# A hybrid encoder layer on one core: four phase borders of an RWKV-7 / attention / gated-convolution kernel, and the order of its gates phase

## The chip, the cores and the metric

One core of a Trainium2 chip. The metric is the device time of one execution in microseconds. A run of this kernel takes about 3.4 ms.

## The reference

The input is x of 2048 tokens by 1024 features, float32, one layer:

```python
h = rms_norm(x)
p = h @ w_in                       # columns: RWKV part (1792), attention part
# RWKV-7, both directions, 8 heads of 64
pf = p + mu_prev*(prev - p) + mu_next*(next - p)
r, k, v, xw, xa, xg = split(pf)
decay = exp(-exp(-softplus(-(w0 + tanh(xw) @ w2)) - 0.5))
iclr  = sigmoid(a0 + xa @ a2);  gate = sigmoid(xg) @ g2
kk = heads(k * k_k);  kk = kk * rsqrt(sum(kk*kk) + 1e-12)
kd = k * (1 + (iclr - 1) * k_a);  b = iclr * kk
S = S*w + (S a) b^T + v k^T;  y = S r     # over 2048 tokens, two directions
y  = group_norm(y_fwd + y_bwd) + bonus;  A = y * gate
# windowed attention (+-128), 8 query heads, 2 kv heads -> B
x = x + concat(A, B) @ w_out
u = conv3(rms_norm(x) @ w_up)      # 2 x 2816 columns, depthwise over tokens
x = x + (silu(u_gate) * u_value) @ w_down
```

## The kernel before

The kernel is a sequence of phases, each a function with its own block of five instruction streams (SyncE for transfers, TensorE, ScalarE, GpSimd, VectorE). Within a phase the order on each engine is written out by hand and the streams meet in counting semaphores (`done(engine, name, n)` waits until `name` has reached n). A phase ends in `end_phase` (L388), which clears its semaphores behind a barrier of all engines. The phases are `first_block` (norm, attention projection), `attention_block`, `rwkv_project_block`, `gates_block`, `recurrence_block`, `mix_block`, `up_block` and `down_block`. Tokens are the free axis nearly everywhere: TN = 4 quarters of NT = 512 tokens, with features on the 128 partitions; RU = 4 is the number of 128-feature tiles of the RWKV width and KD = 8 that of the model width. A matrix product is three float32r matmuls, high by high, low by high and high by low (L91 to L93).

**rwkv_project_block** (L608) makes 14 tiles of 128 columns, in pairs. TensorE does four quarters of a tile, ScalarE copies each quarter to `raw` (L694), VectorE forms the token shift with three operations over all 2048 tokens (L734, L737, L741) and SyncE stores the tile. The last pair holds xw/xa (tile 12) and xg (tile 13). Behind the last tile ScalarE issues eight loads of w0 into row 64 of `lora` (L702), takes tanh of xw and copies xa (L706, L707), and takes the sigmoid of xg (L709).

**gates_block** (L752) runs 32 items: four quarters n, two directions d, four feature tiles. For an item TensorE makes the decay product of a token tile (`p_tok`, L848), the iclr product (`p_iclr`, L851) and, one item later, the running sums of the sigmoids (`p_csum`, L838); ScalarE takes two sigmoids (L885, L889); VectorE makes `keep` (L960), kd (L940) and copies the sums out (L947); GpSimd makes b1 = iclr * kk (L917). `iclr` has three places. Once per quarter the key norm has to be made: GpSimd multiplies keys by k_k (`raw`, L901, 4 operations), ScalarE squares (L870), TensorE sums over heads in pairs (`sums`, L827), ScalarE takes Ln and Exp(-0.5 x) (`roots`, L872) and VectorE multiplies (`unit`, L930). `raw` stands at item 3 of a quarter for the next one, `square` at item 5, and sums, roots and unit at its last item. SyncE stores a quarter's groups in two transfers, 4 MB and 3 MB.

**recurrence_block** (L970) works on 32 chunks of 64 tokens in both directions. A slot c does the state part of chunk c and the preparing part of chunk c + 8. Per group of four chunks the inverses of triangular 32x32 blocks are found by substitution on GpSimd (`solve`, L1072 to L1096) in a transposed layout: VectorE turns the problems (L1480) and turns the results back with two stream transposes (`turn_back`, L1482 to L1487), whereupon ScalarE spreads them (`spread`, L1336). The VectorE order of a slot is a table of stages followed by `turn_back`. At the start VectorE clears buffers and eight PSUM banks (L1410 to L1415), and the other engines wait for all of it.

**mix_block** (L1526) goes in slots of one quarter n and one output tile m: the RWKV result is normed and gated, joined with the attention result, projected, added to x (L1887), stored, squared and summed over tiles on GpSimd (`gather`, L1820) for the next RMS norm (norm on TensorE L1706, root on ScalarE L1772, reciprocal on VectorE L1891). In the last quarter's slots it begins the up phase: SyncE loads quarters 0 and 1 of x back (`load_next`, L1630) into `x_next`, which lies in mix's buffer y; GpSimd scales the eight tiles of a quarter with the reciprocal norm (L1833); ScalarE and VectorE split them into high and low (L1798, L1910, L1914); TensorE makes the first up products of quarter 0 (`up_ahead`, L1717). SyncE loads quarters 2 and 3 in `up_block` (L1965), where GpSimd scales them (L2026).

**up_block** (L1923) takes 22 pairs of a gate tile and a value tile: TensorE four quarters each, ScalarE copies (L2051) and the gate's SiLU (L2057), VectorE three taps per tile (L2108, L2111, L2114), the gate product (L2119) and the value product (L2122), SyncE the store (L1971). **down_block** loads these back.

The wait of ScalarE in the gates is the place that the ring of three sets:

```python
done(act, "iclr_lora", g + 1)
done(act, "b1", g - 2)
done(act, "keep", g - 2)
nc.scalar.activation(iclr[:, g % 3], p_iclr[:, g % 2], ACT.Sigmoid,
                     bias=K.vec("a0", d * RU + j)).then_inc(S["iclr"], 1)
```

## Time and profile before

| | |
|---|---|
| median of 3 runs | 3365.49 us (3362.63 to 3369.56) |
| the profiled execution | 3360.1 us |
| its span | 3358.3 us |
| mean granted clock of TensorE | 0.962 |
| busy, TensorE / VectorE / ScalarE / GpSimd | 91% / 47% / 32% / 23% |
| gates: first VectorE row, last VectorE row | 813.9, 936.2 us |
| recurrence: first VectorE row | 949.3 us |
| up: first matmul | 1886.4 us |
| up: last store | 2861.7 us |

The page's first part gives the busy shares of the whole span; since TensorE is the busiest engine by far, the places to look at are its holes. The part in tenths gives their position by slice of 84 us:

```profile
PE   7878989997847999997899699999999999799999
DVE  4555543333857565543644544444444444333333
ACT  4435541113623444433334221211111121222222
POOL 4434530000625667741224500000000000000000
PEclk9989999998968999998999899999999999899999
DMA  3331122331785333323464211111111111621221
```

### The profile page before, as it was taken

What the parts mean: (1) busy time and instruction counts of PE and PEld (TensorE: products, weight loads), DVE (VectorE), ACT (ScalarE), POOL (GpSimd) and SP (SyncE); (2) the same over time, 40 slices, a digit from 0 to 9 for tenths busy, and PEclk for the clock granted to TensorE, in tenths of its full rate; (3) what the DMA queues carried; (4) which work ended last, traced back from release to release, by engine and by line L of the source; (5) the groups of instructions that cost most, each with busy time, mean ns of one, the idle gap of its engine ahead of it and who ended that gap; (6) DMA issues with size and microseconds to landing.
All of it is one profiled execution on the core that took longest, in us unless ns stands there. A gap on an engine that the chain in (4) does not pass through costs nothing. (4 is left out here: it accounts for less than half of the span.)

```text
span 3358.3 us, 63150 instructions
## 1 busy us (share of the span) xinstructions
PE 3047.4 (91%) x26252; PEld 2446.2 (73%) x26252; DVE 1571.7 (47%) x2023; ACT 1059.4 (32%) x2009; POOL 768.0 (23%) x873
## 2 busy tenths in 40 slices
PE   7878989997847999997899699999999999799999
PEld 4554448885536899996566578888888887688887
DVE  4555543333857565543644544444444444333333
ACT  4435541113623444433334221211111121222222
POOL 4434530000625667741224500000000000000000
PEclk9989999998968999998999899999999999899999
DMA  3331122331785333323464211111111111621221
GB/s 113 132 86 36 38 53 63 75 75 39 286 260 154 114 111 117 99 90 102 157 204 141 91 57 45 49 50 50 50 47 37 47 50 38 247 100 47 99 98 35
DMA packets 229906, 317.57 MB, mean 95 GB/s; under 512 B 80473, under 2 KB 155737, under 8 KB 226738
## 3 DMA queue, kind: packets, MB, share of 16 engines
q1 hardware_dynamic: 223634, 308.98, 28.8%
q10 hardware_dynamic: 6048, 5.38, 0.5%
q8 instruction: 167, 2.74, 0.3%
q14 instruction: 57, 0.47, 0.0%
HBM read 211.17 MB, written 103.14 MB: 94 GB/s over the span
## 5 line engine op out<-in xcount | busy, mean ns | idle before, releaser
L91 PE MATMUL up_p<-h_hi,up_w_hi 128*128 128x512 f32 x1408 | 551.8, 392 | 13.5 <-DVE h_lo L2098 8.2
L92 PE MATMUL up_p<-h_lo,up_w_hi 128*128 128x512 f32 x1408 | 550.2, 391 | 0.0
L93 PE MATMUL up_p<-h_hi,up_w_lo 128*128 128x512 f32 x1408 | 550.2, 391 | 0.0
L2051 ACT COPY up_raw<-up_p 128x512 f32<-128x512 f32 x176 | 103.2, 588 | 758.6 <-PE up_p L93 750.1
L91 PEld LDWEIGHTS up_p<-h_hi,up_w_hi 128*128 128x128 f32 x1408 | 266.0, 189 | 71.2 <-issue 13.2
L92 PEld LDWEIGHTS up_p<-h_lo,up_w_hi 128*128 128x128 f32 x1408 | 266.0, 189 | 56.0 <-issue 0.5
L93 PEld LDWEIGHTS up_p<-h_hi,up_w_lo 128*128 128x128 f32 x1408 | 265.7, 189 | 55.4
L2108 DVE TENSOR_SCALAR up_con<-up_raw,vecs_sb 128x2048 f32<-128x2048 f32 x44 | 59.3, 1347 | 515.8 <-ACT up_raw L2051 515.8
L91 PE MATMUL down_p<-down_act_hi,down_w_hi 128*128 128x512 f32 x704 | 274.6, 390 | 23.5 <-DVE down_act_lo L2252 23.5
L92 PE MATMUL down_p<-down_act_lo,down_w_hi 128*128 128x512 f32 x704 | 274.3, 390 | 0.0
L93 PE MATMUL down_p<-down_act_hi,down_w_lo 128*128 128x512 f32 x704 | 274.3, 390 | 0.0
L2249 DVE TENSOR_TENSOR down_w_lo<-down_w,down_w_hi 128x1024 fp32r<-128x1024 f32 x88 | 107.7, 1224 | 309.8 <-ACT down_w_hi L2231 309.8
L2231 ACT CAST down_w_hi<-down_w 128x1024 fp32r<-128x1024 f32 x88 | 92.8, 1055 | 353.2 <-PE down_p L93 334.6
L91 PE MATMUL p_rwkv<-h_hi,rwkv_project_w_hi 128*128 128x512 f32 x448 | 175.2, 391 | 10.2 <-DVE rwkv_project_w_lo L716 10.2
L92 PE MATMUL p_rwkv<-h_lo,rwkv_project_w_hi 128*128 128x512 f32 x448 | 175.0, 391 | 0.0
L93 PE MATMUL p_rwkv<-h_hi,rwkv_project_w_lo 128*128 128x512 f32 x448 | 175.0, 391 | 0.0
L91 PEld LDWEIGHTS down_p<-down_act_hi,down_w_hi 128*128 128x128 f32 x704 | 132.5, 188 | 51.3 <-issue 23.9
L92 PEld LDWEIGHTS down_p<-down_act_lo,down_w_hi 128*128 128x128 f32 x704 | 132.5, 188 | 27.7
L93 PEld LDWEIGHTS down_p<-down_act_hi,down_w_lo 128*128 128x128 f32 x704 | 132.4, 188 | 27.5
L529 POOL TENSOR_SCALAR attention_prob<-attention_prob,attention_inv 128x384 f32<-128x384 f32 (+1 forms) x96 | 117.1, 1236 | 120.6 <-DVE attention_inv L595 120.6
L584 DVE CUSTOM_DVE_ANT_0 attention_s<-attention_p_s,attention_bias,attention_nsink 128x384 f32<-128x384 f32 (+1 forms) x128 | 75.9, 594 | 108.5 <-PE attention_p_s L492 89.3
L1094 POOL TENSOR_TENSOR rec_V<-rec_V,rec_part 128x31 f32<-128x31 f32 (+15 forms) x217 | 122.2, 563 | 17.0
(244 smaller groups left out, 6324.4 us busy)
## 6 DMA issues: line engine op xcount, KB each, us to landing
rec_inp<-gate_chunks SPq DMA_DIRECT2D x64, 512.0 KB, 3.6
act_out<-up_con SPq DMA_DIRECT2D x22, 1024.0 KB, 4.3
down_act<-act_out SPq DMA_DIRECT2D x88, 256.0 KB, 2.8
up_w<-in_w_up SPq DMA_DIRECT2D x42, 512.0 KB, 4.0
gate_chunks<-gates_out SPq DMA_DIRECT2D x4, 4096.0 KB, 11.8
first_w<-in_w_attn SPq DMA_DIRECT2D x24, 512.0 KB, 3.9
rkv_chunks<-rwkv_project_mix SPq DMA_DIRECT2D x12, 1024.0 KB, 6.5
gate_chunks<-gates_out SPq DMA_DIRECT2D x4, 3072.0 KB, 12.3
```

Source lines behind the costliest of these rows:

```text
L91: pe.matmul(out, w_hi, x_hi, start=start, stop=False)
L92: pe.matmul(out, w_hi, x_lo, start=False, stop=False)
L93: return pe.matmul(out, w_lo, x_hi, start=False, stop=stop)
L529: ops.tensor_scalar(prob[:, i % PB, lo:hi], prob[:, i % PB, lo:hi], inv[:, b % 2, h:h + 1], None, ALU.mult).then_inc(S[name], 1)
L584: nc.vector.tensor_tensor_reduce(s_sb[:, h, lo:hi], p_s[:, i % 3, lo:hi], bias[:, h, lo:hi], 1.0, nsink[:, h:h + 1], ALU.add, ALU.min, lea ...
L1094: op = ops.tensor_tensor(V[:, below, cols], V[:, below, cols], product, ALU.add)
L2051: nc.scalar.copy(raw[:, half, 1 + n * NT:1 + (n + 1) * NT], p_u[:, half, n]).then_inc(S["copied_" + c], 1)
L2108: nc.vector.tensor_scalar(con[:, half], raw[:, half, 1:T + 1], cw(1, half, j), cb(half, j), ALU.mult, ALU.add).then_inc(S["c0" + c], 1)
L2231: nc.scalar.copy(w_hi[:, k % 2], w[:, k]).then_inc(S["w_hi"], 1)
L2249: nc.vector.tensor_tensor(w_lo[:, k % 2], w[:, k], w_hi[:, k % 2].bitcast(F32), ALU.subtract).then_inc(S["w_lo"], 1)
```

## The change

It touches six places.

1. **Projection.** The eight w0 loads are issued by SyncE at the phase's start. Tanh and the copy of xw/xa stand on ScalarE behind the second quarter's copy of tile 13. The shift of tile 13 is done in two pieces, tokens 0 to 1534 and 1535 to 2047, and written to `K.xg` itself; its sigmoid moves to the gates, in four pieces at items 0 to 3.
2. **Gates.** GpSimd squares (one 128x2048 product per quarter), `iclr` has nine places, and fixed tables say at which item the next quarter's key norm is worked on. The ones row is set and copied for the first quarter first and for the rest at item 1. Exp follows each Ln by pairs. The first quarter is saved in seven transfers.
3. **Recurrence, start.** GpSimd clears ring_g, low and side; VectorE clears dec and then the banks, in the order 2, 3, 0, 1; ScalarE waits for dec alone.
4. **Recurrence, turn-back.** `turn_back` stands in front of `state` and `state_decay` in VectorE's slot.
5. **Mix to up.** `x_next` lies in `up_con`; SyncE loads quarter 0 ahead of the slot's store, quarter 1 a slot earlier and quarter 2 still in mix; tiles k with k % 4 < 2 are scaled by GpSimd, the others by VectorE.
6. **Up.** The last pair's value tile is filtered, multiplied and stored in the same two pieces; the SiLU stands in front of the last quarter's copy.

```diff
# rwkv_project_block
+                        if last and b == 1 and n == 1:
+                            act.wait_ge(S["mixed20"], R_TILES // 2)
+                            nc.scalar.activation(K.xw[0:64, :], mix[0:64, 0], ACT.Tanh).then_inc(S["lora_copied"], 1)
+                            nc.scalar.copy(K.xw[64:128, :], mix[64:128, 0]).then_inc(S["lora_copied"], 1)
...
+                    if last and b:
+                        mixed(g, b, m, K.xg, slice(0, T - NT - 1), TN - 1, 1)
+                        mixed(g, b, m, K.xg, slice(T - NT - 1, T), TN, 2)
+                    else:
+                        mixed(g, b, m, mix[:, b], slice(0, T), TN, 1, not first)
# gates_block
-    RAW, SQUARE = 3, 5
+    RAW_AT = {0: 1, ITEMS + 3: 2, 2 * ITEMS + 3: 3}
+    ROOTS_AT = {4: 0, ITEMS + 2: 1, 2 * ITEMS - 1: 2, 3 * ITEMS - 1: 3}
+    SUMS_AT = {5: 0, ITEMS + 2: 1, 2 * ITEMS - 1: 2, 3 * ITEMS - 1: 3}
+    UNIT_AT = {6: 0, ITEMS + 2: 1, 2 * ITEMS - 1: 2, 3 * ITEMS - 1: 3}
+    IRING = 9
...
-                    if i == SQUARE and n + 1 < TN:
-                        square(n + 1)
...
-                    done(act, "b1", g - 2)
-                    done(act, "keep", g - 2)
+                    done(act, "b1", g - IRING + 1)
+                    done(act, "keep", g - IRING + 1)
...
+                    if g < TN:
+                        nc.scalar.activation(K.xg[:, g * NT:(g + 1) * NT], K.xg[:, g * NT:(g + 1) * NT], ACT.Sigmoid)
+                    if g in ROOTS_AT:
                         act.preload_act_table_set("natural_log_exp_and_others")
-                        roots(0)
...
+                        roots(ROOTS_AT[g])
...
                     op.then_inc(S["kk"], 1)
+                    done(pool, "kk", n + 1)
+                    nc.gpsimd.tensor_tensor(inv[:, :, :], kk[:, :, :], kk[:, :, :], ALU.mult).then_inc(S["sq"], 1)
...
-                nc.vector.memset(row[64:128, :], 1.0).then_inc(S["ones"], 1)
+                nc.vector.memset(row[64:128, 0:NT], 1.0).then_inc(S["ones"], 1)
# recurrence_block
-                act.wait_ge(G["init"], INIT)
+                act.wait_ge(G["dec_set"], 2)
...
+                for d in DIRS:
+                    nc.gpsimd.memset(ring_g[d][:, :, :, 0:BL], 0.0).then_inc(G["init"], 1)
+                    nc.gpsimd.memset(low[d][:, :, :], 0.0).then_inc(G["init"], 1)
+                    nc.gpsimd.memset(side[d][:, :, :], 0.0).then_inc(G["init"], 1)
...
-                                         (ahead, rb_mask, c + 1), (carry, state, c), (carry, state_decay, c)):
+                                         (ahead, rb_mask, c + 1)):
...
                         turn_back((c + 1) // GROUP)
-                    for go, stage, n in ((front, diagonal_a, c + LAG), (front, diagonal_b, c + LAG)):
+                    for go, stage, n in ((carry, state, c), (carry, state_decay, c),
+                                         (front, diagonal_a, c + LAG), (front, diagonal_b, c + LAG)):
# mix_block
-        x_next = y.rearrange("p j c m t -> p (j c m t)").rearrange("p (k t) -> p k t", t=NT)
+        x_next = K.up_con.rearrange("p h t -> p (h t)").rearrange("p (k t) -> p k t", t=NT)
...
-                    if s == AHEAD + 4:
+                    if s == AHEAD + 3:
                         done(sp, "h0_lo", KD)
                         load_next(1)
+                for i in range(2):
+                    done(sp, "h1_lo", 4 * i + 4)
+                    sp.dma_start(x_next[:, 4 * i:4 * i + 4],
+                                 K.x2_dram.rearrange("m p t -> p m t")[:, 4 * i:4 * i + 4, toks(2)]).then_inc(
+                        K.rows_in[f"in{i}"], 16)
...
+                    if s == SLOTS - 1:
+                        for k in range(KD):
+                            if k % 4 >= 2:
+                                scale(1, k)
# up_block
+                            if last and half and n == TN - 1:
+                                gate(j)
                             take(half, j, n)
-                    gate(j)
+                    if not last:
+                        gate(j)
...
+                    gated(j)
+                    if last:
+                        for nth, (at, quarters) in enumerate(((EARLY, TN - 1), (LATE, TN)), 1):
+                            taps(1, j, at, quarters, nth)
+                            product_out(j, at, nth)
```

GpSimd's order in the gates, before (L905 is the product with k_k, L917 is b1):

```order
L905 TENSOR_TENSOR gates_kk<-gates_keys,vecs_sb 128x512 x4
L917 TENSOR_TENSOR gates_out<-gates_iclr,gates_out 128x8x64 x3
L905 TENSOR_TENSOR gates_kk<-gates_keys,vecs_sb 128x512 x4
L917 TENSOR_TENSOR gates_out<-gates_iclr,gates_out 128x8x64 x8
L905 TENSOR_TENSOR gates_kk<-gates_keys,vecs_sb 128x512 x4
L917 TENSOR_TENSOR gates_out<-gates_iclr,gates_out 128x8x64 x8
L905 TENSOR_TENSOR gates_kk<-gates_keys,vecs_sb 128x512 x4
L917 TENSOR_TENSOR gates_out<-gates_iclr,gates_out 128x8x64 x13
```

and with the change (L925 the product, L930 the square, L939 b1):

```order
L925 TENSOR_TENSOR gates_kk<-gates_keys,vecs_sb 128x512 x4
L930 TENSOR_TENSOR gates_inv<-gates_kk 128x2048
L925 TENSOR_TENSOR gates_kk<-gates_keys,vecs_sb 128x512 x4
L930 TENSOR_TENSOR gates_inv<-gates_kk 128x2048
L939 TENSOR_TENSOR gates_out<-gates_iclr,gates_out 128x8x64 x11
L925 TENSOR_TENSOR gates_kk<-gates_keys,vecs_sb 128x512 x4
L930 TENSOR_TENSOR gates_inv<-gates_kk 128x2048
L939 TENSOR_TENSOR gates_out<-gates_iclr,gates_out 128x8x64 x8
L925 TENSOR_TENSOR gates_kk<-gates_keys,vecs_sb 128x512 x4
L930 TENSOR_TENSOR gates_inv<-gates_kk 128x2048
L939 TENSOR_TENSOR gates_out<-gates_iclr,gates_out 128x8x64 x13
```

The second group's product and square now stand in front of the first b1, and four squares are new.

VectorE in a slot of the recurrence with a turn-back, before:

```order
L1433 TENSOR_TENSOR rec_akrk<-rec_bank,rec_masks 128x512 x2
L1439 TENSOR_TENSOR rec_rb<-rec_bank,rec_masks 128x256 x2
L1453 TENSOR_TENSOR rec_H<-rec_bank,rec_H 128x256 x2
L1460 TENSOR_TENSOR rec_H<-rec_H,rec_dec_end 128x256 x2
L1486 STREAM_TRANSPOSE rec_upper<-rec_V 128x32x32
L1487 STREAM_TRANSPOSE rec_lower<-rec_V 128x32x32
L1466 TENSOR_SCALAR rec_E<-rec_bank,rec_masks 128x128 x2
```

and with the change:

```order
L1457 TENSOR_TENSOR rec_akrk<-rec_bank,rec_masks 128x512 x2
L1463 TENSOR_TENSOR rec_rb<-rec_bank,rec_masks 128x256 x2
L1510 STREAM_TRANSPOSE rec_upper<-rec_V 128x32x32
L1511 STREAM_TRANSPOSE rec_lower<-rec_V 128x32x32
L1477 TENSOR_TENSOR rec_H<-rec_bank,rec_H 128x256 x2
L1484 TENSOR_TENSOR rec_H<-rec_H,rec_dec_end 128x256 x2
L1490 TENSOR_SCALAR rec_E<-rec_bank,rec_masks 128x128 x2
```

The two transposes changed places with the state's four operations.

VectorE at the end of mix, before (L1887 adds x, L1910 and L1914 make the low parts, L1891 is the reciprocal):

```order
L1891 RECIPROCAL inv_all<-inv_all 128x512
L1887 TENSOR_TENSOR mix_x<-mix_p_out,mix_x 128x512 x3
L1910 SCALAR_TENSOR_TENSOR h_lo<-mix_y,vecs_sb,h_hi 128x512 x4
L1896 TENSOR_TENSOR up_w_lo<-up_w,up_w_hi 128x1024
L1887 TENSOR_TENSOR mix_x<-mix_p_out,mix_x 128x512
L1910 SCALAR_TENSOR_TENSOR h_lo<-mix_y,vecs_sb,h_hi 128x512 x4
L1896 TENSOR_TENSOR up_w_lo<-up_w,up_w_hi 128x1024
L1887 TENSOR_TENSOR mix_x<-mix_p_out,mix_x 128x512 x2
L1914 SCALAR_TENSOR_TENSOR h_lo<-mix_y,vecs_sb,h_hi 128x512 x8
L1891 RECIPROCAL inv_all<-inv_all 128x512
```

and the last part of it with the change (L1925 adds x, L1930 scales):

```order
L1961 SCALAR_TENSOR_TENSOR h_lo<-up_con,vecs_sb,h_hi 128x512 x4
L1925 TENSOR_TENSOR mix_x<-mix_p_out,mix_x 128x512
L1961 SCALAR_TENSOR_TENSOR h_lo<-up_con,vecs_sb,h_hi 128x512 x4
L1944 TENSOR_TENSOR up_w_lo<-up_w,up_w_hi 128x1024
L1925 TENSOR_TENSOR mix_x<-mix_p_out,mix_x 128x512
L1944 TENSOR_TENSOR up_w_lo<-up_w,up_w_hi 128x1024
L1925 TENSOR_TENSOR mix_x<-mix_p_out,mix_x 128x512
L1930 TENSOR_TENSOR up_con<-up_con,inv_all 128x512 x4
L1925 TENSOR_TENSOR mix_x<-mix_p_out,mix_x 128x512
L1965 SCALAR_TENSOR_TENSOR h_lo<-up_con,vecs_sb,h_hi 128x512 x8
L1935 RECIPROCAL inv_all<-inv_all 128x512
```

The four scales of quarter 1 stand on VectorE in front of the last addition of x.

## Rows read from the trace of the kernel before

**Rows 1.** Windows view: busy us (instructions) by engine, granted clock, DMA share, GB/s; gates, recurrence.

```profile
817.00:941.00 124.00, 104.23 (x416) 60.31 (x416) 94.12 (x114) 72.85 (x88) 67.52 (x48) 0.95 0.64 245
1060.00:1565.00 505.00, 474.03 (x14638) 465.55 (x14632) 263.13 (x558) 209.88 (x632) 308.73 (x529) 0.99 0.32 100
```

**Rows 2.** Timeline, end of the projection: start us, us, instruction, [idle before <-releaser].

```profile
800.40 0.59 ACT L694 COPY rwkv_project_raw_pad<-p_rwkv 128x512 f32<-128x512 f32 x1 [4.85 <-PE p_rwkv L93]
800.41 5.14 ACTq L702 DMA_DIRECT2D lora<-in_vecs  x8
804.73 2.35 DVE L741 SCALAR_TENSOR_TENSOR rwkv_project_mix<-rwkv_project_raw_pad,vecs_sb,rwkv_project_mix 128x2048 f32<-128x2048 f32 x1
810.74 1.91 ACT L709 ACTIVATE xg<-rwkv_project_mix 128x2048 f32<-128x2048 f32 x1
```

**Rows 3.** Timeline, start of the gates.

```profile
813.93 1.76 DVE L922 MEMSET gates_row<- 64x2048 f32 x1 [6.85 <-PEq L391]
817.37 1.22 PE L848 MATMUL gates_p_tok<-lora,gates_row 128*128 128x512 f32 x1 [17.01 <-DVE gates_row L928]
```

**Rows 4.** Gates: tile views (duration ns min/median/max) and timeline of TensorE.

```profile
L905 POOL TENSOR_TENSOR gates_kk<-gates_keys,vecs_sb x16: 1040/1217/1487, 819.3 to 899.3; 128x512 f32<-128x512 f32 x16
L917 POOL TENSOR_TENSOR gates_out<-gates_iclr,gates_out x32: 1266/1452/1727, 836.8 to 933.5; 128x512 f32<-128x512 f32 x32
L960 DVE TENSOR_SCALAR gates_keep<-gates_iclr,vecs_sb,gates_less x32: 535/886/1481, 836.6 to 936.2; 128x512 f32<-128x512 f32 x32
...
849.46 1.05 PE L838 MATMUL gates_p_csum<-gates_tri,gates_sig 128*128 128x128 f32 x8
852.07 1.05 PE L838 MATMUL gates_p_csum<-gates_tri,gates_sig 128*128 128x128 f32 x8
```

**Rows 5.** Timeline, start of the recurrence, ACT and TensorE.

```profile
957.39 1.28 ACT L1322 ACT_TABLE_LOAD   x1 [24.02 <-DVE rec_bank L1415]
981.83 1.12 PE L1195 MATMUL rec_bank<-consts_sb,rec_toks 64*64 64x64 f32 x16 [5.41 <-DMA rec_toks<-rkv_chunks]
```

**Rows 6.** Timeline, a slot of the recurrence with a turn-back.

```profile
1106.45 0.25 POOL L1094 TENSOR_TENSOR rec_V<-rec_V,rec_part 128x31 f32<-128x31 f32 x1
1106.60 0.89 DVE L1439 TENSOR_TENSOR rec_rb<-rec_bank,rec_masks 128x256 f32<-128x256 f32 x2 [0.71 <-PE rec_bank L1184]
1111.74 2.01 DVE L1487 STREAM_TRANSPOSE rec_lower<-rec_V 128x1024 f32<-128x1024 f32 x1
1114.83 0.66 PE L1184 MATMUL rec_bank<-rec_side,rec_g 64*64 64x32 f32 x16 [1.12 <-ACT rec_side L1345]
1115.70 0.48 PE L1184 MATMUL rec_bank<-rec_Z,rec_g 64*64 64x32 f32 x10 [0.22 <-ACT rec_side L1345]
```

**Rows 7.** Timeline, end of mix and first wait of up.

```profile
1860.99 12.51 POOL L1833 TENSOR_TENSOR mix_y<-mix_y,inv_all 128x512 f32<-128x512 f32 x8 [4.55 <-DMA mix_y<-x_dram]
1875.23 1.22 PE L1706 MATMUL mix_p_total<-mix_total,consts_sb 128*128 128x512 f32 x1 [15.00 <-POOL mix_total L1820]
1878.06 3.35 DVE L1891 RECIPROCAL inv_all<-inv_all 128x512 f32<-128x512 f32 x1 [2.34 <-ACT inv_all L1772]
1886.42 0.47 PE L91 MATMUL up_p<-h_hi,up_w_hi 128*128 128x512 f32 x1 [2.29 <-DVEq L2087]
1891.41 1.29 POOL L2026 TENSOR_TENSOR up_con<-up_con,inv_all 128x512 f32<-128x512 f32 x1 [16.24 <-DMA up_con<-x_dram]
1906.67 0.77 PE L91 MATMUL up_p<-h_hi,up_w_hi 128*128 128x512 f32 x1 [7.49 <-DVE h_lo L2098]
```

**Rows 8.** Timeline, end of up, and the page's DMA issues (KB each, median us to landing).

```profile
2851.06 1.35 DVE L2108 TENSOR_SCALAR up_con<-up_raw,vecs_sb 128x2048 f32<-128x2048 f32 x1 [15.64 <-ACT up_raw L2051]
2861.74 0.35 SPq L1971 DMA_DIRECT2D act_out<-up_con  x1
2873.86 0.79 PE L91 MATMUL down_p<-down_act_hi,down_w_hi 128*128 128x512 f32 x1 [23.45 <-DVE down_act_lo L2252]
act_out<-up_con SPq DMA_DIRECT2D x22, 1024.0 KB, 4.3
```

More of the change, by code:

```diff
@@ L865, in _ @@
                               K.d["masks"][:, at:at + 2 * P]).then_inc(S["w_in"], 16)
-                def square(n):
-                    done(act, "kk", n + 1)
-                    done(act, "kn", n)
-                    nc.scalar.activation(inv[:, :, :], kk[:, :, :], ACT.Square).then_inc(S["sq"], 1)
                 def roots(n):
@@ L916, in _ @@
                     out_free(pool, n)
-                    nc.gpsimd.tensor_tensor(out[:, n % 2, :, group(f"b1_{d}") + u, :], by_chunk(iclr[:, g % 3]),
+                    nc.gpsimd.tensor_tensor(out[:, n % 2, :, group(f"b1_{d}") + u, :], by_chunk(iclr[:, g % IRING]),
                                             out[:, n % 2, :, group("kk") + u, :], ALU.mult).then_inc(S["b1"], 1)
@@ L951, in _ @@
                 dve.wait_ge(S["less"], 1)
-                for n in range(TN):
-                    copy_row(n)
+                copy_row(0)
                 for g, (n, i, d, u) in enumerate(items):
-                    if g == 0:
-                        sums_out(0, *items[0])
-                        unit(0)
+                    if g == 1:
+                        nc.vector.memset(row[64:128, NT:], 1.0).then_inc(S["ones"], 1)
+                        for m in range(1, TN):
+                            copy_row(m)
+                    if i == 0:
+                        dve.wait_ge(S[f"k_in{n % 2}"], 16 * (n // 2 + 1))
                     done(dve, "iclr", g + 1)
                     done(dve, "kd", g - 1)
-                    nc.vector.tensor_scalar(keep[:, g % 2], iclr[:, g % 3], K.vec("k_a", u), less[:, u:u + 1],
+                    nc.vector.tensor_scalar(keep[:, g % 2], iclr[:, g % IRING], K.vec("k_a", u), less[:, u:u + 1],
                                             ALU.mult, ALU.add).then_inc(S["keep"], 1)
                     times_k(g, n, i, d, u)
-                    if g >= 1:
-                        sums_out(g, n, i, d, u)
-                    if i == ITEMS - 1 and n + 1 < TN:
-                        unit(n + 1)
+                    sums_out(g, n, i, d, u)
+                    if g in UNIT_AT:
+                        unit(UNIT_AT[g])
         end_phase(nc, S)
@@ L1784, in _ @@
                     stage(s, square)
-                    for k in ahead(s, 2):
+                    for k in ahead(s, 1):
                         done(act, "with_bonus", TN * RU)
-                        done(act, "x0_scaled", k + 1)
+                        scaled_ahead(act, 0, k)
                         nc.scalar.activation(K.h0_hi[:, k], x_next[:, k], ACT.Copy,
@@ L1907, in _ @@
                     stage(s, centre)
-                    for k in ahead(s, 3):
+                    for k in ahead(s, 1):
+                        if k % 4 >= 2:
+                            scale(0, k)
+                    for k in ahead(s, 2):
                         done(dve, "h0_hi", k + 1)
```

209 lines of the change are left out of this document (119 added, 90 removed).

## The prediction

> **What bounds the kernel now.** I read the page's tenths by slice first, then the windows view of the stretches that the change touches, then the timeline around each place where TensorE sits idle. The profiled execution took 3360.1 us (span 3358.3), 5.4 us under the median of the three runs shown, 3365.49; I add the sum up against the profiled execution and carry the difference over. TensorE is busy 91% of the span, so what can be won lies in its holes. In the recurrence its matmuls cover 474 of 505 us, in the gates 104 of 124 us [rows 1], and at the border of mix and up it stands still for 15.00 us [rows 7]. The changed borders stand on the chain in full: phases end in a barrier.
>
> **Projection to gates.** The last copy stands at 800.40, 4.85 us behind the one before, and DVE filters the last tile from 801.0 to 804.73 + 2.35 = 807.1. Meanwhile ACT issues eight small loads for 5.14 us, then does tanh, a copy, a table load and the sigmoid, which ends at 810.74 + 1.91 = 812.65 [rows 2], and gates begins 1.3 us behind it [rows 3]. The change issues the loads at the start on SP, where the first tiles' loads stand behind 5.14 us of issuing; a tile is over 20 us of TensorE, which covers it. Tanh and copy move to the last tile, behind its second quarter's copy: 3.8 us on ACT between copies 5.44 us apart (4.85 + 0.59). Three quarters of the taps are done ahead of the last copy (4.5 us within the same 5.44); behind it stand 513 columns, 6.1/4 = 1.5 us and some 0.15. DVE ends near 802.65 in place of ACT at 812.65: **-10.0 us**. The sigmoid of xg goes into gates as four pieces of 0.6 us on ACT.
>
> **Gates.** The first matmul waits for the ones and four row copies, 3.4 us behind DVE's start [rows 3]; a quarter of the memset and one copy leave about 1.1, so it begins 2.1 us earlier. From there an item costs TensorE 2.61 us (852.07 - 849.46), and the 32 items take (936.2 - 836.6)/31 = 3.2 us each [rows 4], because ACT's squares and roots stand between items. If nothing waited, 32 x 2.61 = 83.5, four groups of sums at about 4.6 (two pairs of matmuls with ACT's logarithm between) and 5 us at the ends give 107 against 124 now: 17 us to be had at best. But the squares go to GpSimd as one 128x2048 operation. The rows of before have none; the nearest ones are the key product at 1.04 to 1.49 us and b1 at 1.27 to 1.73 us per 512 columns, undisturbed at the lower ends [rows 4]. Four times these bounds the square by 4.2 and 6.9; I take 4.9, since most of its time has no partner on DVE in the first and last groups. GpSimd then has, per group, 8 x 1.45 + 4 x 1.22 + 4.9 = 21.4 us of work in 26, but in a fixed order, and the order makes waits. By hand from the block's start: the roots of group 0 come behind item 4, and TensorE waits 2.4 us at item 6; the nine places of the iclr ring are full at item 9, so ACT waits there for b1 of item 0, which stands on GpSimd behind the second group's key product and square (34 + 5 + 4.9 = 44 us into the block), about 4 us; b1 then runs behind by about ten items, so the square of group 2, behind 11 of them, is ready near 71 where TensorE wants it near 64, 7 us. Group 3 has room. 107 + 2.4 + 4 + 7 + about 3 for blocking on DVE is 123: **-1 us**, with ends -12 (the b1 at its lowest 1.27, waits of 7 gone) and +8 (b1 at 1.73). The Trainium skill, "SBUF — State Buffer", section "SBUF: two separate sides", says that the port pair of GpSimd and VectorE is an exclusive lock for the whole instruction. The trace is softer for 512 columns: keep is 0.54 us alone, 0.89 at the median and 1.48 at most [rows 4], which fits waiting for the end of one GpSimd operation. By the rule each square would hold DVE for 4.9 us, where I have counted 0.7; that is the rival below. "GPSIMD Engine Reference", section 3.1, gives 4497 ns for a tensor_tensor of 2048 float32 columns; by it the square would cost 0.4 us less than mine, which no run here shows yet.
> The last store's tail, and with it the recurrence's start, hang on the same last item: nothing more there.
>
> **Recurrence, start.** ACT's first step waits for all memsets on DVE and begins at 957.39 [rows 5]. Now it waits for two of 0.07 us, and the others are shared with GpSimd. The input it reads lands about 953 to 954: -3.3 us. A few us on, TensorE waits 5.41 us for a DMA of token rows [rows 5], whose round trips pace these slots; they are also released earlier, so I keep **-3.3**, ends -4 and 0.
>
> **Recurrence, turn-back.** At each of the seven groups' ends DVE transposes 1.96 and 2.01 us behind the state; ACT's spread needs both and TensorE waits 1.12 + 0.22 us for it [rows 6]. In front of the state the transposes could begin when GpSimd has the solve (1106.45 + 0.25) and DVE the masks (1106.60 + 0.89 = 1107.49); they end 2.3 us earlier, at 1111.5 instead of 1111.74 + 2.01. The spread then waits for ACT's y copy only (1112.2), in time. The state ends 3.3 us later, at 1112.9, and the next slot wants it at 1118.4. 7 x 1.34 = **-9.4 us**, rounded down to -9.1 for the tail of the copies; ends -11 and 0.
>
> **Mix to up.** GpSimd scales eight tiles alone (12.51 us from 1860.99 on, after its load), TensorE stands idle 15.00 us until the last gather lets the norm go at 1875.23, DVE's reciprocal is at 1878.06 + 3.35 and up begins at 1886.42 [rows 7]. The load now goes to the buffer of up_con and needn't wait for mix's y; it is issued a slot earlier (about 10 us, of which the slot's work takes some). The scales are split by two engines, four each, and on GpSimd 4 x 1.56 = 6.3 us that lie beside the last slots. TensorE's matmuls end 15.00 us ahead of 1875.23, at 1860.2. I let the gather be done by then and the norm (1.1 us) go at once, the leftover up matmuls run to 1866.6, the reciprocal end at 1868 and up start at 1869.1: **-17.3**. GpSimd then starts the third quarter's scales at once, as its rows are loaded before the barrier; before it waited 16.24 us for them and TensorE 7.49 [rows 7]. Its chain begins 5.0 us earlier after up's start (1891.41 - 1886.42): **-5.0**, together -22.3, ends -25 (all of 7.49 goes) and -15 (DVE's own scales hold its reciprocal back).
>
> **Up to down.** The last pair's filter is a chain on DVE behind the last copy, from 2851.06 to the store at 2861.74; the first down matmul comes at 2873.86, 12.1 us behind the store's issue, of which a store of 1024 KB takes 4.3 us to land [rows 8]. The copies are 5.44 us apart. Now ACT's gate (1.91 us) stands between the third quarter's copy, which ends at 2845.6, and the last one: it ends at 2847.5, DVE's product with it (2.3) at 2849.8, three quarters of the taps (6.05 x 3/4 = 4.5) at 2854.3, their product (1.7) at 2856.0, and the 513 columns behind them take 2.1 + 0.3: 2858.4, a gain of 3.3. The last store is a quarter of the bytes; how much sooner it lands no row shows, between 0 and 4.3 x 3/4 = 3.2 us; I take 1.2. **-4.5**, ends -6.5 and -3.3.
>
> **The sum.** -10.0 - 1 - 3.3 - 9.1 - 22.3 - 4.5 = -50.2 us: 3360.1 - 50.2 = 3309.9 profiled, 3365.5 - 50.2 = **3315** as a median.
>
> **The rivals.** (a) The waits in gates don't arise, because GpSimd runs near its lower ends (b1 1.27, square 4.2): gates gives 11 instead of 1, 3305. For it: alone, the operations are that short [rows 4]. Against it: DVE is busy 94 of the 124 us [rows 1], so GpSimd is seldom alone. Chance 0.20. (b) The square takes the ports for its whole length: four times about 4 us of DVE more, on the path in two or three of them, and b1 later by as much: +8 instead of -1, 3324. For it: keep's spread of 0.54 to 1.48. Against: no row has DVE held for longer than one operation of 512 columns, and the next square falls into DVE's slack. The skill's lock rule from above is this case. Chance 0.15. (c) The recurrence passes nothing on: the start is paced by the DMA's round trips, and the wait for the transposes comes back as one for the state. 12.4 us lost: 3327.6. For it: the 5.41 us wait [rows 5]. Against: after the transposes the state has 5 us to spare. Chance 0.10. (d) The other side: the solve on GpSimd. In front of the state, the transposes hold the state and its decay behind the solve, whose last step ends at 1106.45 + 0.25 [rows 6], 0.8 us ahead of the moment when DVE wants it. Were the solve late, every us beyond 0.8 + 4.2 (the state's slack) would be one on the path, seven times, for GpSimd's order is unchanged. To eat 50.2 us it must be late by 5 + 1.3 + 50.2/7 = 13.5 us in each group; by 14.5 it gives 3373. Nothing in the trace delays it so far (309 of 505 us busy on GpSimd [rows 1]): 0.02. That the change doesn't do what it says is no case of its own: the order on each engine shows every move.
>
> **How the numbers follow.** The forecast, 3315, has 0.53; (a) 0.20, (b) 0.15, (c) 0.10, (d) 0.02. The ends of single terms (mix and up, 7 us to the bad and 4 to the good, gates between) widen each by about 6. From 3301 to 3329 lie the forecast, (a) but for its outer part, (b) and most of (c): a little over 8 in 10. A measurement of this kernel tells apart about 0.2%, 6.7 us. Only a loss of 45 us beyond the forecast would bring it there: same 0.02, slower 0.03, faster 0.95.
>
> **What would show it.** In the profile after: gates' first DVE row near 803.9; in gates a GpSimd row of 128x2048 x4 near 4.9 us, ACT or TensorE waiting at item 9 and before the third sums, and a length near 123; no TensorE wait for the spread of over 0.5 us behind a turn-back, and slots without one as long as before; the idle stretch at mix and up at 1 to 3 us and the first wait of up below 3; the last store of up near 7.4 us behind the last copy's end. Wrong it would be if gates takes under 115 or over 130, if the solve's end moves with the transposes, or if DVE's reciprocal stands behind its scales.

## The result and the profile after

| | before | after |
|---|---|---|
| median | 3365.49 us (5 runs, 3355.24 to 3370.78) | 3338.19 us (5 runs, 3332.21 to 3338.81) |
| profiled execution (span) | 3360.1 (3358.3) | 3333.1 (3331.3) |
| mean granted clock | 0.962 | 0.965 |

The medians lie 27 us apart; the ratio is 0.9924 with a 95% interval of 0.9908 to 0.9939, so the time fell by 0.76%. The forecast was 50 us, and the result lies 9 us above the upper end of its range. Split at rows that both traces have, the profiled executions stand so:

| stretch | before | after | difference | forecast |
|---|---|---|---|---|
| start to the projection's last copy | 800.4 | 801.2 | +0.8 | 0 |
| last copy to gates' first VectorE row | 13.5 | 3.7 | -9.9 | -10.0 |
| that row to the recurrence's first | 135.3 | 153.4 | **+18.1** | -1 |
| that row to the last y copy | 615.0 | 601.1 | -14.0 | -12.4 |
| last y copy to up's first matmul | 322.1 | 310.0 | -12.1 | -17.3 |
| up's first matmul to down's | 987.5 | 977.0 | -10.4 | -9.5 |
| the rest | 484.4 | 485.0 | +0.6 | 0 |

One row is wrong by 19 us, of a miss of 23. The first rows are the projection's end on VectorE. Its last piece of 513 tokens now ends at 803.85, where ScalarE's sigmoid ended at 812.65 [rows 2], and gates begins 1 us behind it, at 804.83 instead of 813.93 [rows 3]:

```profile
803.10 0.75 DVE L748 SCALAR_TENSOR_TENSOR xg<-rwkv_project_raw_pad,vecs_sb,xg 128x513 f32<-128x513 f32 x1
804.83 0.48 DVE L944 MEMSET gates_row<- 64x512 f32 x1 [0.98 <-PEq L391]
```

The windows view of gates, columns as in [rows 1]:

```profile
804.00:947.00 143.00, 113.34 (x416) 63.38 (x416) 101.69 (x119) 70.62 (x93) 81.12 (x52) 0.89 0.58 209
```

Against [rows 1] TensorE does the same 416 matmuls in 113.3 instead of 104.2 us, at a mean granted clock of 0.89 instead of 0.95, and 29.7 us without a matmul stand where there were 19.8. Half of this growth of 19 us are waits, and the other half matmuls behind them at the lower of the clock's two levels, 1.2 instead of 2.4 GHz (from 883.1 to 891.4 us the mean granted clock is 0.52). The longer waits of TensorE on its timeline:

```profile
821.72 1.13 PE L867 MATMUL gates_p_csum<-gates_tri,gates_sig 128*128 128x128 f32 x8 [2.62 <-DVE gates_out L969]
836.27 1.91 PE L867 MATMUL gates_p_csum<-gates_tri,gates_sig 128*128 128x128 f32 x8 [2.49 <-ACT gates_sig L907]
853.99 3.44 PE L860 MATMUL gates_p_ss<-gates_inv,consts_sb 128*128 128x512 f32 x4 [4.46 <-POOL gates_inv L930]
859.63 3.08 PE L860 MATMUL gates_p_ss<-gates_inv,consts_sb 128*128 128x512 f32 x4 [2.20 <-ACT gates_inv L898]
883.03 3.78 PE L860 MATMUL gates_p_ss<-gates_inv,consts_sb 128*128 128x512 f32 x4 [6.67 <-POOL gates_inv L930]
888.02 3.50 PE L860 MATMUL gates_p_ss<-gates_inv,consts_sb 128*128 128x512 f32 x4 [1.21 <-ACT gates_inv L898]
913.87 1.13 PE L867 MATMUL gates_p_csum<-gates_tri,gates_sig 128*128 128x128 f32 x8 [2.23 <-DVE gates_out L969]
```

They name three engines. The sums at 853.99 and 883.03 waited for the square on GpSimd (4.46 and 6.67 us), and the rows behind a wait show the clock: eight running-sum matmuls in 1.91 us at 836.27 where a row at full clock has 1.05 [rows 4], four sums in 3.44 to 3.78 where one at full clock takes 1.98. Two of ScalarE's long waits are for the sums of the first quarter, and in front of item 9's sigmoid for a free place in the ring:

```profile
828.91 1.11 ACT L898 ACTIVATE gates_inv<-gates_p_ss,vecs_sb 128x1024 f32<-128x1024 f32 x1 [7.78 <-PE gates_p_ss L860]
855.24 0.69 ACT L911 ACTIVATE gates_iclr<-gates_p_iclr,vecs_sb 128x512 f32<-128x512 f32 x1 [9.44 <-POOL gates_out L939]
```

VectorE in the same phase:

```profile
810.45 1.37 DVE L984 TENSOR_SCALAR gates_keep<-gates_iclr,vecs_sb,gates_less 128x512 f32<-128x512 f32 x1 [4.48 <-DMA gates_keys<-rkv_chunks]
815.62 4.17 DVE L950 COPY gates_row<-xw 64x512 f32<-64x512 f32 x3
880.04 3.22 DVE L984 TENSOR_SCALAR gates_keep<-gates_iclr,vecs_sb,gates_less 128x512 f32<-128x512 f32 x1
908.24 3.22 DVE L984 TENSOR_SCALAR gates_keep<-gates_iclr,vecs_sb,gates_less 128x512 f32<-128x512 f32 x1
```

The first keep waits 4.48 us for the keys' load, with item 0's running sums, which TensorE needs two items later, queued behind it. Of the three late row copies, which the profile merges into one row, the first takes 3.51 us and the other two 0.41 each; the early one took 0.42. The long one begins 0.4 us behind the first square (815.24 to 818.84). Two keeps of normally 0.54 us, begun beside the third and the fourth square, take 3.22 each. So in three of the four squares one VectorE operation is held until the square is over, and two of TensorE's waits, 2.62 us at 821.72 and 2.23 at 913.87, are for running sums that VectorE copies out behind such an operation. GpSimd's order, the middle of the phase:

```profile
844.98 5.28 POOL L925 TENSOR_TENSOR gates_kk<-gates_keys,vecs_sb 128x512 f32<-128x512 f32 x4 [26.14 <-DVE gates_out L956]
850.34 3.60 POOL L930 TENSOR_TENSOR gates_inv<-gates_kk 128x2048 f32<-128x2048 f32 x1
853.89 11.10 POOL L939 TENSOR_TENSOR gates_out<-gates_iclr,gates_out 128x512 f32<-128x512 f32 x8
869.20 4.53 POOL L939 TENSOR_TENSOR gates_out<-gates_iclr,gates_out 128x512 f32<-128x512 f32 x3 [4.21 <-DVE gates_out L956]
873.68 5.29 POOL L925 TENSOR_TENSOR gates_kk<-gates_keys,vecs_sb 128x512 f32<-128x512 f32 x4
879.05 3.93 POOL L930 TENSOR_TENSOR gates_inv<-gates_kk 128x2048 f32<-128x2048 f32 x1
```

The square takes 3.60 to 3.93 us, less than either end of my estimate. But product, square and eight b1 come in that order, the first b1 starts 49 us into the phase, and the third product at 873.68 has eleven b1 in front of it.

At mix and up, the rows are of GpSimd, TensorE, VectorE and twice TensorE:

```profile
1850.39 6.88 POOL L1850 TENSOR_TENSOR up_con<-up_con,inv_all 128x512 f32<-128x512 f32 x4 [1.93 <-DMA up_con<-x_dram]
1858.80 1.12 PE L1741 MATMUL mix_p_total<-mix_total,consts_sb 128*128 128x512 f32 x2 [2.23 <-POOL mix_total L1861]
1863.86 3.34 DVE L1935 RECIPROCAL inv_all<-inv_all 128x512 f32<-128x512 f32 x1
1869.27 0.47 PE L91 MATMUL up_p<-h_hi,up_w_hi 128*128 128x512 f32 x1 [3.87 <-DVEq L2147]
1897.43 0.47 PE L91 MATMUL up_p<-h_hi,up_w_hi 128*128 128x512 f32 x1 [3.66 <-DVE h_lo L2158]
```

[rows 7] had 15.00 us of waiting for the gather, now it is 2.23; the reciprocal, ready to go near 1863.0, starts at 1863.86 behind eight low parts, and up's first long wait is 3.66 us instead of 7.49. At the end of up (ScalarE, VectorE, TensorE) the first down matmul comes 18.3 us behind the last copy's end, against 22.8 in [rows 8]:

```profile
2827.41 0.59 ACT L2108 COPY up_raw<-up_p 128x512 f32<-128x512 f32 x1 [3.04 <-PE up_p L93]
2835.39 0.69 DVE L2186 TENSOR_TENSOR up_con<-up_con 128x513 f32<-128x513 f32 x1
2846.30 0.79 PE L91 MATMUL down_p<-down_act_hi,down_w_hi 128*128 128x512 f32 x1 [18.93 <-DVE down_act_lo L2324]
```

### The profile page after: what moved, and what is told of

The parts are those of the page before. It is cut to its first block and busy times, and to the rows that moved or that the text cites. A ratio compares the mean times of both kernels' runs of the same rounds, so it can differ in the third digit from the quotient of the medians.

```text
span 3331.3 us, 63159 instructions
## 1 busy us (share of the span) xinstructions
PE 3048.5 (92%) x26252; PEld 2443.2 (73%) x26252; DVE 1575.8 (47%) x2033; ACT 1053.2 (32%) x2012; POOL 774.0 (23%) x875
## 5 line engine op out<-in xcount | busy, mean ns | idle before, releaser
L2170 DVE TENSOR_SCALAR up_con<-up_raw,vecs_sb 128x2048 f32<-128x2048 f32 (+2 forms) x45 | 59.5, 1323 | 497.9 <-ACT up_raw L2108 497.8
## 6 DMA issues: line engine op xcount, KB each, us to landing
down_w<-in_w_down SPq DMA_DIRECT2D x22, 512.0 KB, 13.5
```

The lines of the kernel that those rows point to most:

```text
L2170: nc.vector.tensor_scalar(con[:, half, at], raw[:, half, here], cw(1, half, j), cb(half, j), ALU.mult, ALU.add).then_inc(S["c0" + c], 1)
```

## The experiments

Theory **order**: the tables of the new gates phase make GpSimd, ScalarE and TensorE wait for each other in a loop (product, square, sums, roots, unit, next product), and the square is but one link. Theory **square**: the long GpSimd operation, with its hold on VectorE, costs this in any place. In front of both stood the question whether the phase is at fault at all. Phase lengths below are from the start of VectorE's first gates row to the end of its last (before 124.2, after 142.3 us); the 936.2 us that the section on the profile before gives for the last row are the start of the last keep, and the last row ends at 938.1. The kernel before was measured again beside each group of experiments: 3358.95 us beside e1 to e4, 3356.95 beside e5 to e8, 3358.51 beside e9 to e11 and 3361.75 beside e12, up to 8.5 us below the 3365.49 beside the changed kernel. Between groups, therefore, the ratios are compared and not the microseconds.

**e1, the old gates phase in the changed kernel.** `gates_block` of before, with one addition:

```diff
+                    if g < TN:
+                        nc.scalar.activation(K.xg[:, g * NT:(g + 1) * NT], K.xg[:, g * NT:(g + 1) * NT], ACT.Sigmoid)
```

> The changed kernel with the gates phase of before put back (the sigmoid of xg added in four pieces). If the new gates phase is what went wrong, the time falls by the 18 us by which that phase grew (142.3 instead of 124.2 us from its first VectorE row to its last): 3338 - 18 = 3320 us, and the phase lasts 124 to 127. Rival: the phase is long for something that stands outside it (earlier start, transfers of the phase before, the clock): then it stays near 140 with the old order too, and the time at 3335 to 3338.

Measured 3319.24 us, ratio 0.9880 (0.9861 to 0.9898); phase 125.8 us. The window of it:

```profile
805.00:930.00 125.00, 105.17 (x416) 60.79 (x416) 95.81 (x118) 75.94 (x93) 67.88 (x48) 0.95 0.63 238
```

The clock is back at 0.95 and the matmuls at 105 us. The other five parts are worth 1.20%, 40 us of the 3358.95 measured beside it (34 to 47 by the interval), 9 less than the forecast's 49. The new gates phase costs the difference of the two ratios, 0.44% or 15 us.

**e2, the new gates phase alone**, in the kernel before (without the sigmoid of xg, which stays in its projection).

> The kernel before with the new gates phase alone. Same two theories: if the phase itself costs 18 us, 3365.5 + 18 = 3383 us (a us or two less, since its keys are loaded in the same way); if the cost comes from the border in front of it, 3365.

Measured 3377.03 us, ratio 1.0060 (1.0041 to 1.0079), slower than before: 18 us above the 3358.95 beside it, as the first theory said; phase 137.6 us. The phase itself costs, 13 of the 18 us of its length even without the earlier border.

**e3, squares on ScalarE, all else as changed.**

```diff
+    SQUARE_AT = {3: 0, ITEMS + 1: 1, 2 * ITEMS - 1: 2, 3 * ITEMS - 1: 3}
...
+                    if g in SQUARE_AT:
+                        square(SQUARE_AT[g])
...
-                    nc.gpsimd.tensor_tensor(inv[:, :, :], kk[:, :, :], kk[:, :, :], ALU.mult).then_inc(S["sq"], 1)
```

> The changed kernel with the squares back on ScalarE (1.9 us each, in front of items 3, 9, 15 and 23), all else in the new gates phase as it is. Theory 'order' (the tables make GpSimd, ScalarE and TensorE wait for each other; the square only lengthens one link): two to three of four groups gain the difference 3.7 - 1.9 and the first b1 comes 3.7 us sooner, so 5 to 8 us off, phase 134 to 137, 3331 us. Theory 'square' (the long GpSimd operation with its hold on VectorE's port is the cause): nearly all 18 us go, phase 124 to 127, 3320 us.

Measured 3322.17 us, ratio 0.9887 (0.9870 to 0.9904); phase 127.8 us, 14.5 less: more than the difference of two durations, twice what "order" said and 0.8 us from what "square" said.

```profile
804.00:931.00 127.00, 107.35 (x416) 61.57 (x416) 92.84 (x119) 76.74 (x97) 66.52 (x48) 0.93 0.65 235
```

**e4, other tables, squares on GpSimd.**

```diff
+    RAW_AT = {0: 1, 8: 2, 16: 3}
+    ROOTS_AT = {4: 0, 11: 1, 18: 2, 25: 3}
+    SUMS_AT = {4: 0, 11: 1, 18: 2, 25: 3}
+    UNIT_AT = {4: 0, 11: 1, 18: 2, 25: 3}
...
+                    if n == 1:
+                        done(sp, "kd", 2 * ITEMS)
+                        done(sp, "kk", 2)
+                        load(3)
...
-                    if g == 1:
+                    if g == 0:
+                        sums_out(0, *items[0])
+                    if g == 5:
                         nc.vector.memset(row[64:128, NT:], 1.0).then_inc(S["ones"], 1)
...
```

> The changed kernel, squares on GpSimd as they are, other numbers in the tables: the products with k_k directly behind the b1 that they need (items 0, 8, 16), sums, roots and unit at items 4, 11, 18, 25, the three later row copies at item 5 instead of 1, item 0's sums copied first, the fourth quarter's keys loaded as soon as their place is free. Theory 'order': with the waits gone the phase lasts 115 to 122 us, 20 to 27 less: 3311 to 3318 us. Theory 'square': the squares cost the same in any place, the phase stays above 135: 3330 us or more.

Measured 3321.05 us, ratio 0.9887 (0.9871 to 0.9904); phase 126.3 us, 16 less, between the two expectations. All four squares are on GpSimd here, and each still holds one VectorE operation, so the hold alone is not the cause. Either mending alone takes nearly all of the loss: it was the squares in that order. The windows view shows the new bound, VectorE with 109.5 of 126 us, and the tile view of its operations (duration ns min/median/max) why:

```profile
806.00:932.00 126.00, 104.68 (x416) 59.90 (x416) 109.54 (x119) 70.64 (x93) 83.47 (x52) 0.95 0.63 230
```

```profile
L988 DVE TENSOR_SCALAR gates_keep<-gates_iclr,vecs_sb,gates_less x32: 535/880/3819, 813.9 to 930.3; 128x512 f32<-128x512 f32 x32
L963 DVE TENSOR_TENSOR gates_out<-gates_keep,gates_keys x32: 691/1636/3972, 814.8 to 930.9; 128x512 f32<-128x512 f32 x32
```

A keep of 0.54 us lasts up to 3.82 and a kd of 0.69 up to 3.97 us: as long as one whole square (3.66 to 3.93 us here). The copies of the running sums, whose source is in PSUM (where TensorE's results stand), stay at 0.68 to 0.69 us in every run. The Trainium skill, "SBUF — State Buffer", section "SBUF: two separate sides", calls the port pair that VectorE and GpSimd share an exclusive lock for the whole instruction; these rows agree with it.

**e5 and e6, the new tables in halves** (one execution each, so their phases are compared and not their times): e5 is e4's change at the start of the phase (roots, sums, unit of quarter 0 at items 3, 4, 4; the row copies at item 5), e6 its products at items 8 and 16 with the earlier load.

> The changed kernel with the start of the gates alone mended: roots, sums and unit of the first quarter at items 3, 4 and 4 instead of 4, 5 and 6, the later row copies at item 5, item 0's sums copied first; the products with k_k of quarters 2 and 3 stay at items 11 and 19. Theory 'order': the first unit comes 8 to 10 us earlier (it began 37.5 us into the phase), the later links are unchanged, so the phase of 142 us loses 8 to 10: 132 to 134. Theory 'square' (each square costs its length wherever it stands): unchanged within 3 us.

> The changed kernel with the products and squares of quarters 2 and 3 moved from items 11 and 19 to items 8 and 16 (three b1 of 4.5 us earlier), and the fourth quarter's keys loaded as soon as their place is free. Theory 'order': the waits for the squares of quarters 2 and 3 (6.7 us of TensorE, and ScalarE behind it) shrink by 4.5 us each: phase 133 to 136. Theory 'square': unchanged within 3 us.

Measured 3330.88 us with a phase of 138.7, and 3315.7 us with a phase of 134.4 (e6 had the shortest recurrence of all, see below). TensorE's wait for the third square stays in e5 (first row) and shrinks in e6 (second row):

```profile
880.71 3.78 PE L860 MATMUL gates_p_ss<-gates_inv,consts_sb 128*128 128x512 f32 x4 [6.53 <-POOL gates_inv L930]
```

```profile
874.88 1.98 PE L861 MATMUL gates_p_ss<-gates_inv,consts_sb 128*128 128x512 f32 x4 [1.91 <-POOL gates_inv L931]
```

e5 gained 3.6 of the 8 to 10 us expected, nearer to what "square" said. The first unit came 28 us into the phase instead of 38, but the square of quarter 1 then held a keep for 3.81 us, and TensorE waited 6.48 us for the running sums behind it, in place of 4.46 for the square itself; the third square's wait was untouched. e6 gained 8, as "order" expected. Together they give 11.5, and e4, which also moves sums and roots, 16.

**e7, each square in four pieces** (one execution):

```diff
-                    nc.gpsimd.tensor_tensor(inv[:, :, :], kk[:, :, :], kk[:, :, :], ALU.mult).then_inc(S["sq"], 1)
+                    for u in range(RU):
+                        op = nc.gpsimd.tensor_tensor(inv[:, u], kk[:, u], kk[:, u], ALU.mult)
+                    op.then_inc(S["sq"], 1)
```

> The changed kernel with each square in four GpSimd operations of 512 columns. If VectorE is held for the length of one GpSimd operation, its longest keep falls from 3.22 us to at most 1.5 us; GpSimd itself gets slower (4 x 1.1 to 1.3 = 4.4 to 5.2 instead of 3.6 to 3.9). Theory 'order': the chain through the square is 1 us longer, phase 142 to 146. Theory 'square' by its hold on the port: phase 130 to 136.

Measured 3324.93 us, phase 138.6 us: neither range. The longest keep is 1.37 us, so the hold is one operation long. GpSimd's four pieces take 4.0 to 5.2 us together, and TensorE's waits for the second and third squares grow from 4.46 and 6.67 to 4.89 and 7.58 us. The phase is 3.7 us shorter all the same, which fits a shorter hold: the 2.23 us wait in front of the last sums is gone, and TensorE's matmuls take 110.5 instead of 113.3 us; the early wait of 2.62 us stays, at 2.83. By this one execution the hold is a small share of the 18 us.

```profile
L986 DVE TENSOR_SCALAR gates_keep<-gates_iclr,vecs_sb,gates_less x32: 536/660/1370, 810.1 to 941.0; 128x512 f32<-128x512 f32 x32
L931 POOL TENSOR_TENSOR gates_inv<-gates_kk x16: 1036/1216/1482, 814.9 to 910.8; 128x512 f32<-128x512 f32 x16
```

**e8, new tables and squares on ScalarE** (in front of items 3, 10, 17, 24).

> The new tables (products at items 0, 8, 16; sums, roots, unit at 4, 11, 18, 25) with the squares on ScalarE in front of items 3, 10, 17, 24. With the tables and the squares on GpSimd the phase took 126.3 us with VectorE busy 109.5 of them, held for up to 3.97 us by a square. Theory 'VectorE is the bound there, lengthened by the squares': 4 x 3 us less of it, phase 114 to 120, 3308 to 3314 us. Rival: ScalarE, which must wait for the product before it can square, takes the gain back: 124 to 128, 3319 to 3323 us.

Measured 3312.36 us (3301.44 to 3318.08), ratio 0.9859 (0.9831 to 0.9887); phase 120.5 us, half a us above the first expectation, with a time inside it. It has the lowest ratio of all and beats both kernels; from e1, whose interval overlaps its own, it can't be told.

```profile
804.00:925.00 121.00, 105.47 (x416) 60.98 (x416) 96.59 (x119) 76.95 (x97) 68.16 (x48) 0.94 0.68 248
```

**e9, the turn-back behind the state again**, on e1: the two stages back in the first table.

> The kernel of e1 (all of the change but the gates phase; 3319 us) with the two transposes back behind the state. Theory 'the order of the turn-back is worth its TensorE wait': waits for the spread 13 us again instead of 6, the stretch from the first y to the last back from about 490 to about 499 us, 3328 us. Rival: the shorter stretch is scatter from run to run (it lay between 484 and 497 us with the same code): no more than 3 us, 3319 to 3322.

Measured 3324.65 us, ratio 0.9901 (0.9878 to 0.9923); e1's 0.9880 lies inside this interval. The stretch from first y to last y is 498.3 us (e1 490.8, before 502.0), as the first theory said. Who waits for the spread's tile (us, times), in the changed kernel and in e9:

```profile
  PE rec_bank L1207: 6.1, 1
```

```profile
  PE rec_bank L1193: 13.1, 12
```

The one wait left is the first group's, before the steady slots. One pair of executions can't tell 7 us here from scatter, but the profiles taken together do better: the three with the turn-back behind the state (before, e2, e9) have 502.0, 496.1 and 498.3 us, mean 498.8, and the eleven with it in front 484.3 to 497.0, mean 490.7. The 8 us between the means fit the 7 us of waits that are gone.

**e10, the recurrence's start as before**, on e1.

> The kernel of e1 with the recurrence's start as before (all clearing on VectorE, everybody waits for it). Theory 'the start passes on': the first decay step is 3.5 to 4.3 us later behind VectorE's first row, and the first y as much: 3322 to 3323 us. Rival: the loads of token rows pace the first slots and swallow it: the first y stands at the same distance, 3319.

Measured 3318.63 us, ratio 0.9880 (0.9859 to 0.9901), the same as e1. Behind the first row of the recurrence the first decay step comes at 9.4 us (e1 7.1), the first y at 111.4 (110.7): of 2.4 us 0.7 are left, and TensorE waits five times for token rows in these slots either way (3.4 to 6.2 us each). By this pair the rival was right. But e1 has the latest first y of the eleven profiles with the new start, which lie at 108.2 to 110.7 us, mean 109.4; the three with the old start (before, e2, e10) have 113.0, 113.3 and 111.4, mean 112.6. So the start passes on some 2 to 3 us, too little for the time of a whole execution to show.

**e11, all sixteen scales on GpSimd**, on e1.

```diff
-                        if k % 4 < 2:
-                            scale(0, k)
+                        scale(0, k)
```

(the same for quarter 1; VectorE's are dropped)

> The kernel of e1 with all sixteen scales of quarters 0 and 1 back on GpSimd; buffer, loads and all else stay. It tells the earlier load from the sharing: if the load brought the 12 us at this border, they stay (from the last y to up's first matmul 309 to 311 us, 3319); if the sharing did, the stretch grows by four scales of GpSimd, some 6 us, to 316 (3325).

Measured 3331.57 us, ratio 0.9916 (0.9896 to 0.9936). The stretch from last y to up is 315.4 us (e1 309.8), and TensorE waits for the gather again:

```profile
1838.51 12.59 POOL L1835 TENSOR_TENSOR up_con<-up_con,inv_all 128x512 f32<-128x512 f32 x8 [2.31 <-DMA up_con<-x_dram]
1852.82 2.08 PE L1726 MATMUL mix_p_total<-mix_total,consts_sb 128*128 128x512 f32 x2 [10.34 <-POOL mix_total L1846]
```

12.59 us for eight scales in a row, as before; 10.34 us of waiting instead of 15.00. Of the 12 us won at this border, 5.6 are the sharing and the rest, by subtraction, the earlier load. The whole rose by 12 us against e1 and by 13 against e10, measured beside it, 7 more than this stretch shows: 2.0 to 2.4 each in front of the gates, in the recurrence and in up, of which the first two have the same code and are scatter.

**e12, half of the running sums copied by ScalarE**, on e8: items of odd number, with a semaphore for each engine.

```diff
-                    done(pe, "csum_out", g - 1)
+                    done(pe, f"csum_out{g % 2}", g // 2)
...
+            copy = nc.scalar.copy if g % 2 else nc.vector.tensor_copy
```

> The kernel of e8 (new tables, squares on ScalarE; phase 120.5 us, 3312 us) with the running sums of every second item copied out by ScalarE instead of VectorE: 16 x 0.68 = 11 us less for VectorE, 10 more for ScalarE. If VectorE sets the steady item of 2.9 us there, the phase falls to 113 to 117 us and the time to 3305 to 3309. Rival: ScalarE with roots, squares and copies becomes the bound and the phase stays at 119 to 124, 3311 to 3316.

Measured 3320.24 us, ratio 0.9879 (0.9862 to 0.9895), which overlaps e8's: the two can't be told apart. The phase fell to 116.9 us as expected, but the recurrence starts 131.3 us behind the phase's first row, in e8 132.0. Windows of its end:

```profile
910.00:920.00 10.00, 9.16 (x48) 6.10 (x47) 9.86 (x11) 5.89 (x10) 7.63 (x6) 1.00 1.02 401
920.00:930.00 10.00, 0.00 (x0) 0.00 (x0) 1.74 (x3) 0.00 (x0) 0.00 (x0) 0.60 1.02 402
930.00:936.00 6.00, 0.00 (x0) 0.00 (x0) 0.00 (x0) 0.00 (x0) 0.00 (x0) 0.50 0.70 275
```

The engines are done at 921.8 and the transfers go on for another 12 us, until 930 at a share of 1.0 and 400 GB/s; the recurrence begins at 936.2. The bound is now the store.

## Why the prediction was wrong, point by point

**Projection to gates**: right, -9.9 for -10.0, by its own steps; VectorE ends 0.4 us later behind the last copy than counted, and the barrier is 0.3 us shorter.

**Gates**: wrong, and with it the total; the length of 142.3 us is also past the 130 that the forecast named as its sign of being wrong. The step that failed is the hand schedule, "107 + 2.4 + 4 + 7 + about 3 for blocking on DVE is 123", and in it above all the 107, which has every matmul at full clock. Its 32 x 2.61 and four groups of 4.6 us, less a wait of 1.2 in each, are by this estimate some 97 us of matmuls; TensorE's own rows say 113.3 us for these 416. The kernel before needs 104.2 [rows 1], so 7 of the 16 us were on record already. What the phase adds are the matmuls behind the new waits. The time without a matmul, some 26 us in the forecast, is 28.9 of the phase's 142.3 us.

The waits that make up this sum came out unevenly. Two were right: TensorE's at item 6 (2.49 us for 2.4) and in front of the third sums (6.67 for 7). The ring's wait, put at 4 us, is 9.44 on ScalarE, and TensorE meanwhile waits 4.46 for the second square, for which no wait was counted. Both come from the start, which was taken as free: the second group's product begins 40 us into the block instead of 34 and the first b1 at 49 instead of 44, because the keys land 4.48 us after VectorE wants them, in front of the running sums, because a row copy is held for 3.51 us, and because ScalarE stands 7.78 us in front of the first roots. The third quarter's square was ready at 78 in place of 71. The price of the square was wrong in the other direction, 3.6 to 3.9 instead of 4.9 us. The Trainium skill's 4497 ns ("GPSIMD Engine Reference", section 3.1) for a GpSimd tensor_tensor of 2048 float32 columns, there an add, is nearer than mine and still above what these runs show for a product with both inputs the same. With the right duration the forecast of the phase would have been still lower.

The rival (b), +8 for the hold on the ports, named a mechanism that the changed kernel shows in three of its four squares and e4 in all four (up to 3.8 and 4.0 us for one operation); in e7, with the hold cut to one short operation, the phase is 3.7 us shorter. No case held a loss of 18: the range of the term ended at +8, since I took its waits as nearly independent and gave them no price in clock. That the loop multiplies a late link is what e3 suggests, where a square of 1.9 us in place of 3.6 to 3.9 gave back 14.5; but e3 also ends the hold and frees GpSimd, and how the 18 us split over these is not shown.

**Recurrence**: -14.0 for -12.4. The mechanism of the turn-back is right: TensorE's wait went from 13.4 to 6.1 us, and what is left is the first group's, which the move doesn't touch. Its size was read from one group's 1.34 us and multiplied by seven; the six other groups together gave 7.3 us of waits instead of the 9.4, and the profiles taken together 8. The start gave 2 to 3 us of its 3.3, of which the pair e10 and e1 shows only 0.7; rival (c) is not borne out. The -14.0 of this one pair of profiles are -3.7 ahead of the first y and -10.3 behind it, where the execution of before is the longest of all: the rest is scatter as far as is known.

**Mix to up**: -12.1 for -17.3. "I let the gather be done by then" failed by 3.6 us (a wait of 2.23, and the matmuls themselves ending 1.4 later), and the reciprocal's end, counted 4 us too early, has eight low parts in front of it. The forecast had allowed for this: the end of its range was -15 for this border and up's first wait together, and -12.1 - 3.8 = -15.9 came. The earlier start of up's scales gave 3.8 of the 5.0 us forecast (7.49 to 3.66).

**Up to down**: right, -4.5 for -4.5; VectorE ends 8.1 us behind the copy where 7.4 stood, and what follows is as much shorter. Together with the 3.8 us from up's start these are 8.3 of the 10.4 us that the row from up to down shows; where the other 2.1 come from is open.

## What to carry to other kernels

When an operation moves to another engine, draw the loop that it stands in and ask how often it runs in one period. Here each mending alone (a shorter link, or the link put directly behind what it needs) gave back 14 to 16 of 18 us. Price every new wait of TensorE twice: its length, and the matmuls behind it that run at the lower clock. Look for single long operations in rows that the profile merges: the copy of 3.51 us hid in a mean of 1.39. And before an engine is relieved, look at what stands next to it in the same stretch: at 117 us the gates were bound by their store.

## What the runs showed of the hardware that was not expected

- One 128x2048 product on GpSimd with both inputs the same takes 3.60 to 3.93 us, four of 128x512 take 4.0 to 5.2.
- VectorE operations with SBUF operands, 0.54 and 0.69 us alone, took up to 3.82 and 3.97 us beside a GpSimd operation of 3.66 to 3.93; with pieces of 1.2 us the longest were 1.37 and 1.65. Those with a source in PSUM stayed at 0.68 to 0.69.
- The steady part of the recurrence, with the same code, took 484.3 to 497.0 us in eleven executions (first y to last y), whose mean granted clocks over the whole run were 0.965 to 0.969. This spread is larger than several of the effects measured here. Its cause stays open.
